# Head steps of a hybrid decoder step: a fixed PSUM bank for each kind of job, cached scores ahead of the block transposes, cached mix in the step of its transposes

## The reference, cut to what matters

```python
# prompt: 6 latent (MLA) heads and 6 windowed heads, 256 x 256 causal
p = softmax(q_h @ k_h.T * scale + mask); o_h = p @ v_h
# sample token b of 8, 6 heads, against 2048 cached rows of 128 latent + 32 rope values
s_past = (q_lat[b] @ past_c[b].T + q_rope[b] @ past_r[b].T) * scale
p = softmax(concat([s_past, s_new])); o_lat = p[..., :P] @ past_c[b] + p[..., P:] @ c_new
# sample token b, windowed heads: 3 x 128 gathered keys (dilations 1, 4, 16)
s_win = q[b] . window_keys[b]
```

## Time and profile before

| | |
|---|---|
| times of three runs | 2453.34, 2455.12, 2461.57 us (median 2455.12) |
| the profiled execution | 2448.66 us, of which the span of its instructions is 2446.7 |
| busy in the span | PE 2383.2 us (97%), DVE 1591.0 (65%), ACT 1304.8 (53%), POOL 102.6 (4%) |
| granted TensorE clock, mean | 0.994 of full speed |
| head steps 0 to 11 up to ow(0), first layer | 113.7 to 214.6 us |
| the same, second layer | 1321.0 to 1424.35 us |

### The profile page before, as it was taken

One profiled execution on the slowest core, in us unless ns is written; L12 is line 12 of the kernel. 1 busy time (PEld: TensorE's weight loads), 2 busy tenths in 40 slices (PEclk: granted clock), 3 DMA queues, 4 the chain that ended last, 5 costly groups with the idle time before them and its releaser, 6 DMA issues.

```text
span 2446.7 us, 46258 instructions
## 1 busy us (share of the span) xinstructions
PE 2383.2 (97%) x17270; PEld 2038.4 (83%) x17270; DVE 1591.0 (65%) x3791; ACT 1304.8 (53%) x2915; POOL 102.6 (4%) x140
## 2 busy tenths in 40 slices
PE   6999999999999999999999999999999999999998
PEld 4565689999999988778866657999999999887786
DVE  2375167786677877667734643676857778776776
ACT  1353234545766666666614432345467766666665
POOL 2100010000000000000021000100000000000000
PEclk9999999999999999999999999999999999999999
DMA  7442337776656567676564324477756565676664
GB/s 245 154 141 70 121 136 256 250 257 245 211 192 223 199 216 243 221 235 206 173 204 144 116 72 153 165 256 252 267 208 224 199 216 206 220 228 220 194 192 153
DMA packets 143341, 481.96 MB, mean 197 GB/s; under 512 B 25699, under 2 KB 52385, under 8 KB 139023
## 3 DMA queue, kind: packets, MB, share of 16 engines
q1 hardware_dynamic: 132638, 438.71, 53.0%
q0 software_dynamic: 10496, 40.42, 4.7%
HBM read 475.81 MB, written 104.21 MB: 237 GB/s over the span
## 4 chain that ended last, share of the span: by engine, by line
PE 93%; DVE 3%; SPq 2%; DMA 1%; issue 1%; ACT 0%; DVEq 0%; ACTq 0%
PE ps L1084 30%; PE ps L1130 28%; PE ps L798 12%; PE ps L1074 7%; PE ps L1096 5%; PE ps L763 3%; PE ps L788 1%; PE ps L1059 1%; PE ps L807 1%; DMA big<-in_state_win_k 1%; PE ps L936 1%; PE ps L920 1%; PE ps L923 0%; PE ps L950 0%; PE ps L884 0%
## 5 line engine op out<-in xcount | busy, mean ns | idle before, releaser
L1084 PE MATMUL ps<-parts_hw,parts_uv 128*128 128x256 f32 x6144 | 797.3, 286 | 1.0 <-DVE parts_uv L1965 1.0
L1084 PEld LDWEIGHTS ps<-parts_hw,parts_uv 128*128 128x128 f32 x6144 | 751.6, 192 | 1.9 <-issue 1.6
L1130 PE MATMUL ps<-parts_uv,parts_hw 128*128 128x512 f32 x3072 | 703.3, 391 | 10.5 <-DVE parts_uv L1994 5.8
L1130 PEld LDWEIGHTS ps<-parts_uv,parts_hw 128*128 128x128 f32 x3072 | 578.2, 189 | 137.8 <-issue 11.9
L1994 DVE TENSOR_TENSOR parts_uv<-region,parts_uv 128x512 fp32r<-128x512 f32 x512 | 351.9, 692 | 189.1 <-ACT parts_uv L1378 164.2
L1378 ACT CAST parts_uv<-region 128x512 fp32r<-128x512 f32 x512 | 317.4, 621 | 245.1 <-PE ps L1130 244.0
L1965 DVE TENSOR_TENSOR parts_uv<-ps,parts_uv 128x512 fp32r<-128x512 f32 x512 | 329.2, 685 | 127.5 <-ACT parts_uv L1360 124.9
L1360 ACT CAST parts_uv<-ps 128x512 fp32r<-128x512 f32 x512 | 285.5, 614 | 1.2 <-PE ps L1074 1.2
L1397 ACT ACTIVATE big<-ps 128x256 f32<-128x256 f32 (+26 forms) x256 | 131.6, 514 | 243.0 <-PE ps L1084 242.9
L1074 PE MATMUL ps<-identR,rows_r 128*128 128x128 f32 x2048 | 202.4, 243 | 1.4 <-ACT big L1351 1.4
L1074 PEld LDWEIGHTS ps<-identR,rows_r 128*128 128x128 f32 x2048 | 191.8, 140 | 1.7 <-ACT big L1351 1.7
(11 more groups left out here) (286 smaller groups left out, 1969.2 us busy)
## 6 DMA issues: line engine op xcount, KB each, us to landing
region<-in_peer_u SPq DMA_DIRECT2D x256, 512.0 KB, 3.9
region<-in_peer_v SPq DMA_DIRECT2D x256, 512.0 KB, 4.3
out<-in_state_win_k SPq DMA_DIRECT2D x16, 1536.0 KB, 9.0
out<-in_state_win_v SPq DMA_DIRECT2D x16, 1536.0 KB, 7.2
out<-in_state_win_k SPq DMA_DIRECT2D x16, 1534.5 KB, 9.1
out<-in_state_win_v SPq DMA_DIRECT2D x16, 1534.5 KB, 7.6
region<-in_peer_wq SPq DMA_DIRECT2D x8, 2048.0 KB, 8.6
big<-in_state_win_k SPq DMA_DIRECT2D x48, 192.0 KB, 3.6
```

Source lines behind the costliest of these rows:

```text
L1084: mm = pe.matmul(ps[:, 4 + j % 2, 0:SEQ], uT[j % 2][a][:, 128 * c:128 * c + 128], hp[b][:, c, :], start=(c == 0 and n == 0), stop=(c == KD ...
L1130: mm = pe.matmul(ps[:, 2 * half + t, :], wp[j % UN][a][:, 128 * t:128 * t + 128], vp[j % 2][b][:, 512 * half:512 * half + 512], start=(j = ...
```

## The change

It does four things. Bank numbers in the head steps no longer rotate over all eight: each kind of job has a bank of its own (S 0; PP and PT 1; SC and ol 2; qbc 3; O 4), and the cT and rT groups take turns in banks 5, 6 and 7. TensorE does PP(b) and SC(b) right behind S, ahead of cT and rT. ol(b) runs in the step of PP(b), one step earlier than before. ACT and DVE follow: ACT copies PP first, then takes the exponentials of S and of SC, then copies cT and rT; DVE does its taps ahead of the window scores. SC's move is now told by the semaphore of its exponential ("L").

```diff
@@ job_plan
+        if s - 2 in PAST_STEP:
+            jobs.append((("PP", PAST_STEP.index(s - 2)), "A"))
+        if s - 1 in PAST_STEP:
+            jobs.append((("SC", PAST_STEP.index(s - 1)), "L"))
         if s in PAST_STEP:
             b = PAST_STEP.index(s)
             jobs += [(("cT", b, g), "A") for g in range(4)] + [(("rT", b), "A")]
         if 1 <= s <= 2 * NH:
             jobs.append((("PT", s - 1), "A"))
-        if s - 1 in PAST_STEP:
-            jobs.append((("SC", PAST_STEP.index(s - 1)), "A"))
...
         if s - 2 in PAST_STEP:
-            jobs.append((("PP", PAST_STEP.index(s - 2)), "A"))
-        if s - 3 in PAST_STEP:
-            jobs.append((("ol", PAST_STEP.index(s - 3)), "A"))
+            jobs.append((("ol", PAST_STEP.index(s - 2)), "A"))
...
-BANK = [LATE.get(name, n % 8) for n, (name, _) in enumerate(JOBS)]
+HOME = {"S": 0, "PP": 1, "PT": 1, "SC": 2, "ol": 2, "qbc": 3, "O": 4}
+PAST_TURNS = [name for name, _ in JOBS if name[0] in ("cT", "rT")]
+
+
+def bank_of(n, name):
+
+    if name in LATE:
+        return LATE[name]
+    if name[0] in HOME:
+        return HOME[name[0]]
+    if name[0] in ("cT", "rT"):
+        return 5 + PAST_TURNS.index(name) % 3
+    return n % 8
+
+
+BANK = [bank_of(n, name) for n, (name, _) in enumerate(JOBS)]
...
-        moved = {"V": moved_v, "A": moved_a}
+        moved = {"V": moved_v, "A": moved_a, "L": [lexp_ready] * DEPTH}
...
@@ vector engine
+                    for n in range(5):
+                        k = next(taps, None)
+                        if k is not None:
+                            tap(k)
                     if s < NB:
                         window_scores(s)
                     if s == NB - 1:
                         window_new()
-                    for n in range(5):
-                        k = next(taps, None)
-                        if k is not None:
-                            tap(k)
```

More of the change, by code:

```diff
@@ L962, in _ @@
                         scores(s)
+                    if s - 2 in PAST_STEP:
+                        turn_past_probs(PAST_STEP.index(s - 2))
+                    if s - 1 in PAST_STEP:
+                        score_past(PAST_STEP.index(s - 1))
                     if s in PAST_STEP:
@@ L966, in _ @@
                         turn_probs(s - 1)
-                    if s - 1 in PAST_STEP:
-                        score_past(PAST_STEP.index(s - 1))
                     if s < NB:
@@ L973, in _ @@
                     if s - 2 in PAST_STEP:
-                        turn_past_probs(PAST_STEP.index(s - 2))
-                    if s - 3 in PAST_STEP:
-                        mix_past(PAST_STEP.index(s - 3))
+                        mix_past(PAST_STEP.index(s - 2))
                     if s == WINDOW_STEP[0]:
@@ L1263, in _ @@
                 for s in range(2 * NH + 2):
+                    if s - 2 in PAST_STEP:
+                        b = PAST_STEP.index(s - 2)
+                        o = read("PP", b)
+                        act.copy(PPs[:, b % 2, :, :].rearrange("p c k -> p (c k)"), o[:, 0:512]).then_inc(moved_a[now[0]], 1)
+                    if s < 2 * NH:
+                        wait_moved(act, "S", s)
+                        for i, c0 in ((0, 0), (1, 128)):
+                            pr_ = prob[:, s % 2, c0:c0 + 128 * (i + 1)]
+                            e = act.activation(pr_, pr_, ACT.Exp, bias=nmx[:, s, i:i + 1], scale=-1.0, accum_out=den[:, s, i:i + 1])
+                        e.then_inc(exp_ready, 1)
+                    if s - 1 in PAST_STEP:
+                        b = PAST_STEP.index(s - 1)
+                        o = arrive(act, "SC", b)
+                        act.wait_ge(nms_ready, b + 1)
+                        if b >= 1:
+                            act.wait_ge(product[now[0]], NUM["PP", b - 1] + 1)
+                        act.activation(Pm, o[:, 0:512], ACT.Exp, bias=nms[:, b:b + 1], scale=SA, accum_out=dens[:, b:b + 1]).then_inc(lexp_ready, 1)
                     if s in PAST_STEP:
@@ L1272, in _ @@
                         act.copy(rT.rearrange("p g k -> p (g k)"), o[:, 0:512]).then_inc(moved_a[now[0]], 1)
[L1273 to L1278, removed]
                     if 1 <= s <= 2 * NH:
@@ L1281, in _ @@
                         act.copy(probT[:, (s - 1) % 2, :], o[:, 0:384]).then_inc(moved_a[now[0]], 1)
[L1282 to L1290, removed]
                     if s - 2 in PAST_STEP:
                         b = PAST_STEP.index(s - 2)
[L1293 to L1296, removed]
                         o = read("ol", b)
```

## The result

| | before | after |
|---|---|---|
| median of six runs | 2460.56 us (2453.34 to 2464.15) | 2478.39 us (2467.93 to 2480.39) |
| profiled execution | 2448.66 us, clock 0.994 | 2467.93 us, clock 0.993 |
| busy in the span: PE, DVE, ACT | 2383.2, 1591.0, 1304.8 us | 2390.2, 1592.2, 1307.1 us |

The ratio is 1.0076, with a 95% interval of 1.005 to 1.0101: the change costs 0.8%. By the medians that is 17.8 us, from profiled execution to profiled execution 19.3 us, where the prediction had 16.7. The prediction named 2472 us, counted from a median of 2455.12; six runs of the kernel before have 2460.56, which is most of the distance to 2478.39. As with the kernel before, the profiled execution was the quickest shown; the other five runs of after had a mean clock of 0.987 to 0.990.

A forecast was written before the change was run, and what follows sets the result against it. TensorE was taken to bound the kernel; 18.0 us added per layer, 36.0 in two, less 19.3 taken away, gave +16.7 us: 2465.4 for the profiled execution, 2472 on the median; range 2459 to 2486.

The forecast's parts named there:

- What is taken away: Both layers' head steps: TensorE's waits for O's normalising, 12.5 us, and slow clock behind them, 6.8 us, go; 19.3 us.
- cT's fourth group: Steps 1, 2, 3, 6, 9: with three banks cT(b, 3) waits 1.5 us for ACT's copy, 7.5 us per layer.
- Steps 0, 5 and 8: Head steps with cT but no SC: cT's fourth group waits 1.2, 1.8 and 3.4 us behind the exponentials of S.
- sum for step 3: Head step 3 on TensorE, from the start of S: 11.2 us with the cT wait, against 9.9 before.
- DVE is late: Steps 5 and 8: DVE reaches S(5) 3.3 us and S(8) 3.7 us into the step, lengthening the cT waits.
- The rivals that put the waits below 0.9 us: Head steps: old waits go, new cT waits are hidden; -15 us, 2440 us, chance 0.10.
- DVE in time: Steps 5 and 8: DVE not late, each wait 0.8 us, clock stays up; +6.1 us, 2461 us, chance 0.15.
- Step 4's ol: Head step 4: ol waits 0.2 us for SC's exponential in shared bank 2.
- the fillers of PT(11): End of the head steps: these fillers, now in bank 1, wait 1.4 us for ACT's move of ow(1).
- The clock behind step 8: After step 8's 3.4 us wait, in each layer: the slow clock costs 1.7 us.
- The end of the steps: Fillers of PT(11), owT and O(11) wait 1.4, 0.5 and 0.3 us; 2.2 us per layer.
- the clock rival: Clock falls more often, 1.7 to 3.4 us behind steps 5 and 9; +7 to +14, 2479 to 2486 us, chance 0.15.

The follow-up runs named there:

- e1: Changed kernel with the old rotating banks (job n in bank n % 8), its new order kept; 2438.05 us, ratio 0.9924 to the kernel before.
- e2: Changed kernel, fixed banks kept, with ACT copying cT and rT ahead of the exponentials of S and SC; 2449.44 us, ratio 0.9975 to before.
- e5: Changed kernel with two banks (5 and 6) instead of three for the cT and rT groups; 2493.47 us, ratio 1.0161 to before.
- e3: Changed kernel with PT(10), ow(0), ow(1) and owT moved to banks 3, 5, 6 and 0; 2465.17 us, ratio 1.0037 to before.
- e9: Changed kernel with two filler matmuls ahead of the third group of each cT; 2471.10 us, ratio 1.0079 to before.
- e6: Kernel before with one edit, DVE's taps ahead of the window scores; 2446.26 us, ratio 0.9964 to before.
- e7: Changed kernel with rotating banks and DVE's old order (window scores, then taps); 2446.24 us, ratio 0.9965 to before.
- e8: Changed kernel with rotating banks and ACT's copies of cT and rT ahead of the exponentials; 2459.01 us, ratio 1.0014 to before.
- e4: Changed kernel with both early ACT copies of cT and rT and the four jobs in other banks; 2442.90 us, ratio 0.9939 to before.

## Why the prediction was right, and where its terms were off

- **What is taken away** (19.3 us predicted). The waits for O are gone, 12.5 us, as predicted. The slow clock in the head steps of before, 0.98 and 0.95, had cost 2.0 and 5.2 us, 7.2 in all for the 6.8 predicted; the 2.1 us lost in the second layer of after belong to a term below. e1 gives 18.7 us by the medians, but 10.2 between the two profiled executions, and the 19.3 had been added up from one execution. That these two numbers agree so well is in part luck.
- **cT's fourth group** (1.5 us in steps 1, 2, 3, 6 and 9). Place, releaser and chain were right; each wait cost 1.1. The two links that were too long were read from rows in which ACT did more than here: its wait for its own completion with the no-op behind the exponential, and the hand-over behind another copy. The prediction knew that the no-op goes and put that at under 0.1 us; the link got 0.21 shorter (0.89 to 0.68). Steps 0, 5 and 8 were 1.2, 1.8 and 3.4 in the prediction and are about 0.9, 1.4 and 2.9 (brackets of 0.76, 1.21 and 2.76 with the same 0.17 added). Together that is 10.8 us per layer where the prediction had 13.9. Its sum for step 3 (11.2) came out at 11.08 by luck: without the wait it adds up to 9.65, where the step took 9.89 before. That DVE is late was right: it starts on S(8) 3.4 us into step 8, where 3.7 was predicted. The rivals that put the waits below 0.9 us, or DVE in time, fall. e2 (the copy earlier, waits gone) and e5 (less work in hand, waits longer) show that the chain against the work in hand is the cause.
- **Step 4's ol** (0.2 us): no such wait. The step grew by 0.27 us all the same, in gaps of 0.1 that no wait row names.
- **Missed:** the fillers of PT(10) share bank 1 with PP(7), whose copy they await for 0.7 us (L803 on L1282). The same look at the bank list that found the fillers of PT(11) would have found it.
- **The clock behind step 8** (1.7 us in both layers): 1.7 us in the second layer alone (12.23 against 10.55).
- **The end of the steps** (2.2 us per layer): waits of 1.19, 0.48 and 0.21, 1.9 in all. But the slow clock behind them was not in the sum, 3.5 and 4.7 us more than before. This is the largest error, a term that the sum did not have at all. It is the clock rival's price at a place where it hadn't been looked for: "If steps 5 and 9 are each followed by 1.7 to 3.4 us lost" named the wrong steps.
- **The total** came out 2.6 us short. The head steps were predicted at about 109 us and took 105.7 and 107.4; the end was predicted at +1.2 and took +4.5 and +5.7. The two errors have opposite signs, so the total was right partly by their cancelling. Some 2 us lie in differences of 0.1 to 0.3 us per step that no wait row names. That the two large terms have opposite signs, and that most of the first is ACT's order, is what e1, e2 and e3 show.

**Left open.** When the clock falls is not settled. In after, a wait of 2.76 us left it up in the first layer and was followed by a slow step in the second; 1.2 us of waiting for ow(1) was followed at once by 0.54 in the first and 0.58 in the second, and in e2 and e9 by 3.7 us at 1.00 and only then by 0.60 to 0.67. e3 had a spell in steps 1 and 2 behind waits of under 1 us, and e1 one in step 1 of its first layer (9.14 us against 7.45) with no listed wait near it. The five other runs of after had 0.987 to 0.990, so in most runs more of such spells fell somewhere, and no trace shows where. Step 4 has idle time without a cause in any view: TensorE stands for 0.3 to 1.1 us before or amid the scores of SC in e1, e3, e6 and e7 ("issue"), and ACT starts the copy of ol(1) 2.4 us after ol(1) in after (150.98 to 153.36) and 3.2 in e2 (149.47 to 152.71), which costs e2 its 0.9 us before SC. In after POOL sends off its four gathers of cached ropes (L693) between 149.1 and 153.9; whether that is the cause was not tested.

## What to carry to other kernels

Giving a kind of job its own PSUM banks is a scheduling decision: where it has more groups in a row than banks, add up the chain until the first group is moved out and take off the work in hand (here 2.47 less 1.35 us, eight times a layer), and then go through who had each bank last, job by job, the single jobs at the end of a loop above all. The remedy was either more banks (e1) or the copy ahead of the other work on its engine (e2), but not both (e8), since an engine's order suits one assignment of banks. Change order and banks in separate builds: here they had opposite signs, and the kernel with the lowest ratio, 0.9924, has only one of them. e4 (0.9939), with both and two repairs, can't be told from it.

## What the runs showed of the hardware that had not been expected

- The hand-over from ACT to TensorE was 0.05 us behind ow(1)'s move (228.38 to 228.43) and 0.11 behind a copy of cT, where the prediction took 0.26 from a row of before. An exponential of 128 x 512 let the next instruction start after 0.68 us, and after 0.89 where ACT waited for its own completion and ran a no-op first.
- The same wait of 1.19 us, at the same place, was followed by different clocks: by 0.54 and 0.58 over 3.7 us in the two layers of after and 0.69 in the first of e5, but by 1.00 over 3.7 us in both layers of e2 and e9 and the second of e5. Behind that the clock stood at 0.50 to 0.67 in all of them, up to the output projection. The window of the fillers and PT(11), and the one behind it, in e2:

```profile
222.88:226.55 3.67, 3.19 (x22) 2.08 (x24) 0.42 (x3) 0.48 (x1) 0.00 (x0) 1.00 0.00 0
226.55:235.05 8.50, 8.29 (x59) 7.72 (x56) 1.03 (x5) 1.81 (x5) 0.00 (x0) 0.61 0.01 2
```

- The stretch from ow(0) to owT takes 10.47 us in e3 and e4, without the waits, 12.27 with them where the clock stayed up (e2, e9, second layer of e5), and 13.60 to 13.97 where it fell at once. A wait of 2.76 us, followed by two fillers of 128 x 512 that took 1.88 us, left it at 1.00 in the first layer.
